# Re-ordering the recurrent part, the key norms and the index scores of a two-layer block

## The reference

```python
# recurrent branch: 4 heads of 128, chunks of L = 128 tokens
a = g[..., None] - b + ic;  w_loc = exp(a - a.max(-1))
c_loc = einsum(vc * w_loc, kc)                       # state of a chunk
c_new = s_old * c_st + s_loc * c_n                   # scan over chunks
dmat = where(causal, b[:, None] - b[None, :] + ic, -inf)
m_t = maximum(inter, dmat.max(-1))
sw  = exp(dmat - m_t) * einsum(qc, kc)
num = sw @ vc + s_inter * (qc @ c_prev)              # "total", with the denominator
h   = num / maximum(abs(den), exp(-m_t))
# sparse branch: sk = rope(rms(s_k)), a query keeps its 128 best keys by
rel = relu(einsum(qi, ki));  score = einsum(wi * idx_scale, rel);  topk(score)
# difference branch: dk = rope(rms(d_k)); two softmaxes, p0 - lam * p1, times d_v
```

## Time and profile before

| | before |
|---|---|
| median of three runs | 3195.16 us |
| profiled execution | 3193.1 us, span 3191.3 us |
| TensorE busy | 3024.3 us, 95% |
| VectorE busy | 1519.9 us, 48% |
| ScalarE busy | 615.3 us, 19% |
| GpSimd busy | 1993.1 us, 62% |
| mean granted TensorE clock | 0.979 |

### The profile page before, as it was taken

One profiled execution on the slowest core, in us unless ns is written; L12 is line 12 of the kernel. 1 busy time (PEld: TensorE's weight loads), 2 busy tenths in 40 slices (PEclk: granted clock), 3 DMA queues, 4 the chain that ended last, 5 costly groups with the idle time before them and its releaser, 6 DMA issues.

```text
span 3191.3 us, 38478 instructions
## 1 busy us (share of the span) xinstructions
PE 3024.3 (95%) x14046; PEld 2477.7 (78%) x14046; DVE 1519.9 (48%) x2517; ACT 615.3 (19%) x1354; POOL 1993.1 (62%) x2041
## 2 busy tenths in 40 slices
PE   7978989999999997899999999999999999999998
PEld 6866767888887876677878888777878888888886
DVE  6676773543333776786463333455530221223543
ACT  3253333110001326333110000000010211111000
POOL 6754433777777765444577777676776555555775
PEclk9998999999999999899999999999999999999999
DMA  4321211433333322111243333322333222322332
GB/s 138 99 67 50 60 50 57 129 92 96 100 89 102 117 92 63 47 53 60 74 122 96 95 96 96 96 86 78 98 98 106 75 79 76 96 79 73 92 96 75
DMA packets 87067, 274.65 MB, mean 86 GB/s; under 512 B 10384, under 2 KB 11025, under 8 KB 86929
## 3 DMA queue, kind: packets, MB, share of 16 engines
q1 hardware_dynamic: 85392, 270.71, 28.1%
q10 hardware_dynamic: 1536, 2.10, 0.3%
HBM read 266.48 MB, written 4.19 MB: 85 GB/s over the span
## 4 chain that ended last, share of the span: by engine, by line
PE 86%; DVE 10%; ACT 3%; issue 1%; DMA 0%; SPq 0%; POOL 0%; DVEq 0%; ACTq 0%
PE PS L435 56%; PE PS L484 14%; PE PS L728 4%; PE PS L736 3%; PE PS L789 1%; DVE MSK L1890 1%; DVE SMALLS L1889 1%; PE PS L994 1%; PE PS L766 1%; PE PS L777 1%; ACT MS L1104 1%; PE PS L448 1%; DVE MS L1935 1%; PE PS L969 0%; PE PS L961 0%
## 5 line engine op out<-in xcount | busy, mean ns | idle before, releaser
L397 POOL TENSOR_TENSOR POOL_C<-POOL_C 128x1 f32<-128x1 f32 x538 | 127.9, 238 | 1130.6 <-PE PS L435 604.3
L405 POOL TENSOR_TENSOR WL<-RAW,WH 128x512 fp32r<-128x512 f32 (+2 forms) x538 | 792.6, 1473 | 9.8
L435 PE MATMUL PS<-XNH,WH 128*128 128x512 f32 x1752 | 696.1, 397 | 13.9 <-DVE EYL L1572 9.5
L435 PE MATMUL PS<-XNL,WH 128*128 128x512 f32 x1752 | 686.2, 392 | 0.0
L402 POOL TENSOR_TENSOR WL<-RAW,WH 128x512 fp32r<-128x512 f32 x420 | 575.1, 1369 | 35.0
L398 POOL TENSOR_SCALAR WH<-RAW 128x1024 fp32r<-128x1024 f32 (+3 forms) x538 | 537.9, 1000 | 0.3 <-issue 0.2
L435 PE MATMUL PS<-XNH,WL 128*128 128x512 f32 x1752 | 433.9, 390 | 0.0
L435 PEld LDWEIGHTS PS<-XNH,WH 128*128 128x128 f32 x1752 | 330.7, 189 | 88.9 <-DVE EYL L1572 10.7
L435 PEld LDWEIGHTS PS<-XNL,WH 128*128 128x128 f32 x1752 | 330.7, 189 | 71.5 <-issue 2.9
L435 PEld LDWEIGHTS PS<-XNH,WL 128*128 128x128 f32 x1752 | 327.6, 187 | 68.8
L484 PE MATMUL PS<-WH,XNH 128*128 128x512 f32 x704 | 280.3, 398 | 11.2 <-ACT TB L1104 6.6
(11 more groups left out here) (370 smaller groups left out, 4571.8 us busy)
## 6 DMA issues: line engine op xcount, KB each, us to landing
RAW<-w_oslot SPq DMA_DIRECT2D x56, 512.0 KB, 3.6
RAW<-w_L0ffn SPq DMA_DIRECT2D x44, 512.0 KB, 3.6
RAW<-w_L1ffn SPq DMA_DIRECT2D x44, 512.0 KB, 3.6
RAW<-w_od SPq DMA_DIRECT2D x32, 512.0 KB, 3.6
RAW<-w_epool SPq DMA_DIRECT2D x24, 512.0 KB, 3.6
RAW<-w_eug SPq DMA_DIRECT2D x16, 512.0 KB, 3.6
RAW<-w_eout SPq DMA_DIRECT2D x16, 512.0 KB, 3.6
RAW<-w_ovc SPq DMA_DIRECT2D x16, 512.0 KB, 3.6
```

Source lines behind the costliest of these rows:

```text
L397: nc.gpsimd.tensor_tensor(POOL_C[:, 1:2], POOL_C[:, 0:1], POOL_C[:, 0:1], ALU.add)
L405: nc.gpsimd.tensor_tensor(WL[:, half, at_:w], RAW[:, slot, at_:w], WH[:, half, at_:w].bitcast(F32), ALU.subtract).then_inc(S("weights_spli ...
L435: mm = nc.tensor.matmul(bank, w[:, slot, k * cols:(k + 1) * cols], x[:, k0 + k, :], start=first and j == 0 and w is WH and x is hi, stop=l ...
```

## The change

No arithmetic changes. What moves:

1. `diagonal(0)` goes ahead of ScalarE's reading of the kv-up banks.
2. The totals get two buffers, `total_of(n)`: `TOT` for odd steps, two blocks of `YC` for even ones, and two sets of reciprocals in `AD`. VectorE's wait before L1842 is for the step before the last.
3. In step 2 ScalarE's two copies into `DKR` go ahead of the value weights (`VW`), the turned keys (`KTM`) and the diagonal.
4. The difference keys are scaled by their roots on ScalarE, 32 activations of 128x64, and VectorE's multiply goes.
5. Behind the hidden tiles, TensorE turns the sparse keys (now into banks 0, 1, 4, 5), then the difference keys, then does `index_scores(1)` (banks 6, 7, 4). ScalarE's order follows. The claim of all eight banks before the attention goes.
6. In attention step 0 the index scores come in pairs: behind each half of the gate's high part, behind its low part, and in the middle of the branch chunk. VectorE sums tokens 256 to 383 before it scales the gate, the rest right after, and the four top-8 rounds come last.

```diff
+        def total_of(n):
+            return heads(TOT if n % 2 else YC[:, 2:4, :].rearrange("p a t -> p (a t)")[:, 0:516], 4)
 # TensorE
-                index_scores(1, (0, 1, 4, 5))
                 pe.wait_ge(*L("sk_normed", 1))
-                to_features(... TA ..., 4, (6, 7, 2, 3), ...)
+                to_features(... TA ..., 4, (0, 1, 4, 5), ...)
                 pe.wait_ge(*L("dk_normed", 1))
                 to_features(... DKR ..., 4, (0, 1, 4, 5), ...)
+                index_scores(1, (6, 7, 4))
-                    if a == 0:
-                        claim(0, 1, 2, 3, 4, 5, 6, 7)
...
                             gate_high(name, i, 0)
+                        if indexed:
+                            index_scores(2, (4, 7), (0, 1))
                             gate_high(name, i, 1)
+                        if indexed:
+                            index_scores(2, (4, 7), (2, 3))
                             gate_low(name, i)
-                        if a == 0 and q == 0:
-                            index_scores(2, (4, 7))
-                            index_scores(3, (4, 7))
+                        if indexed:
+                            index_scores(3, (4, 7), (0, 1))
                         if q < 8:
-                            branch(name, i, third_and_fourth if q and a == 1 else None)
+                            branch(name, i, (lambda: index_scores(3, (4, 7), (2, 3))) if indexed else
+                                   third_and_fourth if q and a == 1 else None)
 # ScalarE
                     take((5, 6, 7, 0)[f], SQT[:, f, :], T, f + 6)
+                act.wait_ge(*L("u_ready", 1))
+                diagonal(0)
                 chunk(seg("kvup") + 1)
...
                     run(ARG[...], ARG[...], ACT.Exp, L("pex_ready"))
+                    if n == 2:
+                        chunk(seg("dkA") + 4)
+                        for m in range(2):
+                            run(DKR[:, m, :], PS[4 + m][:, :], ACT.Copy, L("dk_raw"), scale=RTOK[:, m:m + 1])
                     if n < NT - 1:
...
                 root("dk")
+                act.wait_ge(*L("rk_ready", 2))
+                for n in range(NT):
+                    for h in range(S_HEADS):
+                        x = DKR[:, n, h * S_DH:(h + 1) * S_DH]
+                        run(x, x, ACT.Copy, L("k_scaled"), scale=RSH[:, 8 * n + h:8 * n + h + 1])
                 chunk(seg("dv") + 4)
 # VectorE
-                        norm_tile(buf, n, RSH, tables, name)
+                        if name == "dk":
+                            dve.wait_ge(*L("k_scaled", 32 + 8 * n + 8))
+                        norm_tile(buf, n, None if name == "dk" else RSH, tables, name)
...
-                        dve.wait_ge(*L("hall_ready", 4 * n))
+                        since(dve, *L("hall_ready", 4 * n - 4))
...
+                        if a == 0 and q == 0:
+                            index_sum(2)
                         if q < 8:
                             scale_gate(gates_of, q)
+                        if a == 0 and q == 0:
+                            index_sum(3)
                         if a == 0 and q < 8:
                             for r in range(4):
                                 mark_top(4 * q + r)
-                        if a == 0 and q == 0:
-                            index_sum(2)
-                            index_sum(3)
```

More of the change, by code:

```diff
@@ L691, in layer, with index_scores @@
                             lambda f: L("ya_low", f + 1))
-                def index_scores(n, banks):
+                def index_scores(n, banks, of=range(IDX_HEADS)):
                     w = (n + 1) * P
-                    for h in range(IDX_HEADS):
+                    for h in of:
                         b = banks[h % len(banks)]
@@ L1248, in layer, with diagonal @@
                     take((5, 6, 7, 0)[f], SQT[:, f, :], T, f + 6)
+                def diagonal(n):
+                    if n:
+                        act.wait_ge(*L("ub_ready", n))
+                    for h in range(M_HEADS):
+                        run(DG[:, h * P:(h + 1) * P], IDENT[:, :], ACT.Copy, L("diag_ready"),
+                            scale=U[:, 4 * n + h:4 * n + h + 1])
+                act.wait_ge(*L("u_ready", 1))
+                diagonal(0)
                 chunk(seg("kvup") + 1)
@@ L1256, in layer @@
                 root("sk", squares=False)
-                def diagonal(n):
-                    if n:
-                        act.wait_ge(*L("ub_ready", n))
-                    for h in range(M_HEADS):
-                        run(DG[:, h * P:(h + 1) * P], IDENT[:, :], ACT.Copy, L("diag_ready"),
-                            scale=U[:, 4 * n + h:4 * n + h + 1])
                 def scale_keys(n):
@@ L1268, in scale_keys @@
                         x = TA[:, n, h * S_DH:(h + 1) * S_DH]
-                        run(x, x, ACT.Copy, L("sk_scaled"), scale=RSK[:, 8 * n + h:8 * n + h + 1])
+                        run(x, x, ACT.Copy, L("k_scaled"), scale=RSK[:, 8 * n + h:8 * n + h + 1])
                 def hidden_tile(n):
@@ L1274, in hidden_tile @@
                     for h in range(M_HEADS):
-                        run(HALL[:, n, h * P:(h + 1) * P], heads(TOT, 4)[:, h, 0:M_DH], ACT.Copy, L("hall_ready"),
-                            scale=AD[:, 4 + h:5 + h])
-                act.wait_ge(*L("u_ready", 1))
-                diagonal(0)
-                act.wait_ge(*L("rsk_ready", 1))
+                        run(HALL[:, n, h * P:(h + 1) * P], total_of(n)[:, h, 0:M_DH], ACT.Copy, L("hall_ready"),
+                            scale=AD[:, 4 + 4 * (n % 2) + h:5 + 4 * (n % 2) + h])
+                act.wait_ge(*L("rk_ready", 1))
                 scale_keys(0)
@@ L1297, in layer @@
                         diagonal(n + 1)
-                    if n == 2:
-                        chunk(seg("dkA") + 4)
-                        for m in range(2):
-                            run(DKR[:, m, :], PS[4 + m][:, :], ACT.Copy, L("dk_raw"), scale=RTOK[:, m:m + 1])
                     act.wait_ge(*L("swt_ready", n + 1))
```

41 lines of the change are left out of this document (21 added, 20 removed).

## The result

| | before | after |
|---|---|---|
| median | 3193.25 us (4 runs, 3187.85 to 3195.42) | 3167.02 us (4 runs, 3166.85 to 3167.63) |
| span of the profiled execution | 3191.3 us | 3165.1 us |
| mean granted TensorE clock | 0.979 | 0.984 |

The ratio is 0.9921, interval [0.9904, 0.9938]: faster, a gain of 0.8% that is clear of the noise, and inside the range. The gain is 26.2 us where 34.5 were forecast. (The lines of TensorE are 4 higher than before at most places: L621 is L625, L646 is L650, L674 is L678, L736 is L740, L777 is L779. Of VectorE L1771 is L1785, L1842 is L1856 and L1640 is L1652.)

What follows compares the result with a forecast made beforehand. TensorE, holding 86% of the chain of waits, was taken as the bound. Gains of 17.85 us in layer 0 and 16.7 in layer 1, together 34.5, gave a median of 3160 us, range 3149 to 3180.

Steps and rivals of the forecast that it cites:

- main case: Whole kernel: the forecast gains hold and the median falls between 3150 and 3168 us; chance 0.60.
- first diagonal early: Recurrent step 0: exponentials come 2.9 us earlier, less 0.8 us for TensorE's lower clock; net 2.1 us a layer.
- totals and key copies: Recurrent steps 1 and 2: two totals buffers and earlier key copies together gain 7.0 us in layer 0, 5.85 in layer 1.
- V4 to H: From the fourth group of values matmuls to the hidden tiles' transposes: no edit, 0 us forecast.
- roots, transposes, index scores: From the hidden tiles' transposes to attention step 1's second scaled gate: 8.75 us a layer together.
- Two totals buffers: Recurrent step 1: VectorE stops waiting for ScalarE's reading of the totals; TensorE's 0.91 us wait shrinks, gaining 0.85 us.
- Key copies: Recurrent step 2: TensorE's half chunk starts earlier at full clock, gaining 6.15 us in layer 0, 5.0 in layer 1.
- Roots on ScalarE: Difference-key norming: VectorE loses four 0.69 us multiplies, so the keys are ready 1.8 us earlier.
- Transposes first: Before attention step 0: selected-key transposes go under VectorE's norming; attention scores start at 305.4 us, not 310.36.
- Index scores spread: Attention step 0: index pairs among gate and branch work bring step 1's probabilities earlier; 3.75 us of the 8.75.
- Contention moves with the shift: Rival: shorter waits put VectorE's tiles beside GpSimd's splits more often, taking 7 of 17 us a layer: 3175; chance 0.18.
- slower case: Rival: more, shorter gaps keep TensorE at half clock, losing 7 us a layer: about 3209; chance 0.04.

Runs made afterwards that it cites:

- e1: The changed kernel with only its first diagonal put back behind ScalarE's key roots: 3166.02 us, ratio 0.9914.
- e6: The changed kernel, with TensorE made to wait for VectorE's key-root reciprocal before its first half chunk of keys: 3156.81 us, ratio 0.9898.
- e9: e6 with the first diagonal put back behind ScalarE's key roots: 3164.29 us, ratio 0.9911.
- e2: The changed kernel with one totals buffer and VectorE's wait for ScalarE's last reading of it: 3168.57 us, ratio 0.9930.
- e4: The changed kernel with the difference keys multiplied by their roots on VectorE again: 3169.96 us, ratio 0.9932.
- e5: The changed kernel with step 0's index scores in one piece behind the gate chunk and VectorE's sums behind the top-8 rounds: 3167.02 us, ratio 0.9933.
- e8: The changed kernel with ScalarE's index-score Relus written in place in PSUM and VectorE summing from there: 3165.32 us, ratio 0.9922.
- e10: The changed kernel with e6's TensorE wait and e8's in-place Relus together: 3161.34 us, ratio 0.9900.
- e12: e6 with the last index block's sums moved behind the four top-8 rounds: 3155.02 us, ratio 0.9885.

## Why the prediction was right, and where it was not

The sign, the range and the main case held. By the landmarks, forecast and gain a layer (layer 0 / layer 1) are:

| | forecast | measured |
|---|---|---|
| first diagonal early (to V1) | 2.1 / 2.1 | 0.5 / 0.5 |
| totals and key copies (V1 to V4) | 7.0 / 5.85 | 5.6 / 5.1 |
| V4 to H, no edit | 0 / 0 | -0.2 / -1.6 |
| roots, transposes, index scores (H to G) | 8.75 / 8.75 | 7.1 / 7.0 |
| sum | 17.85 / 16.7 | 13.0 / 10.9 |

- *First diagonal early.* This is the term that failed: 2.1 us forecast, 0.5 measured, because its waits left out VectorE's small operations. The start of the maxima was right, and the arguments were to be ready 7.3 us after the zero; they came at 9.5. The prediction counted the meeting with GpSimd for tiles of 256 and 512 columns, and for nothing in the small operations. It did say that the half chunk would be done in the gap, but not that its end starts the split under the maxima. That is 2.1 of the 2.9 us: the turned scores came 0.8 us earlier than before and not 2.9. The clock is the smaller part. The prediction let the 4 us gap cost 0.8 us; it was 6.6 us, and the half clock behind it cost 0.3 us up to V1 and 0.8 in V1's own matmuls. e1 shows the term at 0.5 us by V1 and at nothing in the time, e6 and e9 that the 2.9 us behind it are right once the meeting is gone.
- *Two totals buffers.* 0.85 us, measured 0.9 (e2, within what the same stretch varies by). It does not show in after against before from V1 to V2 (13.7 against 13.4 us) because the half clock behind the 6.6 us gap takes it back: V1's matmuls alone take 1.93 us instead of 1.13.
- *Key copies.* The half chunk waits 0.36 us, the values matmul 0.72 in layer 0 and 0.55 in layer 1. I had VectorE's fourth key-turn instruction beside a split at 0.7 us more; L1652 took 1.56 us instead of 0.69. V2 to V3 fell by 5.9 and 4.9 us, against 6.15 and 5.0.
- *V4 to H.* No edit is here. The 0.2 and 1.6 us lost are within the 27.3 to 30.3 us that this stretch took in all traces.
- *Roots on ScalarE.* Right in mechanism, and 2.35 us instead of 1.8 (e4).
- *Transposes first.* Right: from H to the attention scores I had 13.7 us and it took 13.4, and K's transposes took 3.67 us, as the 3.65 of the earlier trace rows.
- *Index scores spread.* This is the second term that was mis-sized: 3.75 us of the 8.75, and e5 leaves 1.0 and 0.7. The mask ended 30.4 us after H, not 28.0. Of these 2.4 us, 1.3 are the meeting with the split that the gate chunk's end starts (from the first Relu of the last pair to the mask's end 3.86 us, not 2.57); e8, where it is gone, takes 2.54 there. The other 1.1 are a Relu that started later: TensorE reached the last pair 0.5 us late, and the Relu started 1.16 us behind the start of its matmul, where I had 0.55. The rounds took 3.9 us as in the earlier trace rows, and from the maxima to the first turned probabilities it took 2.2 us, not 2.7. TensorE waited 4.40 us, not 3. From H to the first turned probabilities 36.6 us, not 34.6; the 1.5 us for the clock was about right, 3.25 us instead of 2.07 for eight matmuls. The gain of H to G is mostly the roots and the order of transposes and attention scores, for which I had 5 us: e5 keeps them and takes 41.0 us in layer 0 where before took 47.1.
- *The rivals.* "Contention moves with the shift" is what happened, at about half of its price: 2.2 us in the recurrent part and 1.3 us in the index part, of 7. Its reasoning was right, that a shorter wait puts VectorE beside a split; my reason against it, that both shift together, was wrong wherever TensorE does a half chunk inside the gap. The slower case did not come: the clock of the stretch rose from 0.87 to 0.93.

Up to G the gain fell 4.9 and 5.8 us short: 1.6 us a layer for the first diagonal, 1.4 and 0.8 between V1 and V4, 0.2 and 1.6 for the clock between V4 and H, and 1.7 and 1.8 from H to G, where the spreading was 3 us short and the roots and the order gave 1 us more than forecast. The other 2.3 us of the gain, ahead of the zero and outside the layers, are in no term; that they brought the total nearer to the forecast was luck.

## What to carry to other kernels

When an idle engine does queued work early, ask what the end of that work releases: here a weight split on GpSimd, which then stood in the way of the engine that was waited for, so that a wait of 2 us added to TensorE made the kernel 6 to 10 us faster (e10, e6). Count the small instructions too, since each one with two SBUF inputs can cost the whole rest of a GpSimd instruction, here 1.1 us on one of 0.15. And where there is work with time to spare, try it behind the gap: in layer 0 of e6 the half clock fell on it and not on the path, in layer 1 it did not.

## What was new of the hardware

- A VectorE instruction of 128x4 with two SBUF inputs took 1.25 and 1.11 us instead of 0.15 beside GpSimd's 1.26 us instructions, and ended within 0.02 us of their ends. The 128x8 maxima over 256 columns in the four rounds took the same 0.43 us beside a split (e12, rounds from 305.55 to 309.44, split from 305.10 to 308.77) as without one. One tile as input is not enough to be safe: the first sum, a multiply of a 128x512 tile by one number a partition, took 1.29 us beside a split in after and 0.49 without.
- The length of a gap did not decide the clock behind it. TensorE ran at half clock behind gaps of 6.59, 4.40 and 4.02 us, and at full clock behind 1.63 us (e12) and 0.98 us (e6). But behind the same 1.99 us, with the same work before it, it ran at 0.50 in layer 0 of e6 and at 1.00 in layer 1, and behind 3.37 to 3.41 us ahead of V4 at either level or at both in turn. What decides it, no run here shows.
